# The residual rows stored to memory ahead of the experts, and added to there by each expert's scatter

## The chip, the cores and the metric

The program runs on one core of one Trainium2 chip. The time is device microseconds of that core, launch to end of one execution. Measured before the change: a median of 1953.42 us in 3 runs (1949.82 to 1957.47).

## The reference

Two layers (DEPTH = 2) over x, 256 tokens by 2048 numbers, float32. Each layer is an attention part and a mixture of experts (MoE):

```python
x = x + mixed @ w_out[l]
x = x + moe_ffn(rms_norm(x, ffn_norm[l]), w_router, router_bias, w_gate[l], w_up[l], w_down[l])
```

The MoE has 16 experts. The router picks 2 of them for each token, both from one group of 4 experts. An expert computes `silu(h @ wg) * (h @ wu)`, scaled by the token's gate value, and then `@ wd`. A token's result is its x plus the outputs of its two experts. One expert's weights are 3 x 2048 x 512 floats, 12.6 MB; a layer's 16 experts are 201 MB.

## The kernel before, in words

Each layer first streams the weights of the input projection and the output projection through TensorE (PE), with the attention heads worked in between. It ends with the new x in SBUF (tile `x`, two tiles of 128 tokens by 2048) and the normalised rows in `rows`. POOL stores these to memory (`expert_rows`, L508).

Then comes the expert stage, `one_round`. It is written out by hand as a list of steps for each engine.

- SP issues the weight loads (`load`, L460), 192 loads of 1 MB a layer, into a ring of 8 buffers: four in `raw`, four in `proj`. A load waits on `lo_ready`, that is, until both halves of what its buffer held have been cut. The first 8 loads of the stage go out before the attention part has ended.
- Every half buffer is cut into a high part by ACT (L590) and a low part by VectorE (DVE, L1232), and PE multiplies with both (L1032, L1034, L1051 to L1053). So one expert takes 24 cuts on ACT, 24 on DVE and 24 groups of matmuls on PE.
- A round has 64 places (SLOTS) for each expert. POOL gathers an expert's rows from `expert_rows` by the table `tok_at` (L514) and later scatters its results with `put_at` (L522). A row of 2048 numbers is handled as two rows of 1024 (4 KB), so each gather and scatter has 128 places; those without a token point out of bounds and move nothing. With 256 tokens and two picks each, a mean of 32 of an expert's 64 places are filled.
- The scatters write into the tensor `picks`, of 2 x 256 rows: the first picks of all tokens and then the second picks. A row has one writer. 14 of the 16 experts scatter; the last two are joined in SBUF by a matmul (`join`, L1079) and added to `x` from PSUM by `add_last` (L1746). In the attention part POOL fills `picks` with x_in (L499), so that every row holds finite numbers.
- At the end of the stage POOL waits for the sixth and then for the last of the final 8 weight loads (`raw_landed5`, `raw_landed7`) and loads `picks` back, four tiles of 1 MB (L560). DVE multiplies each by a mask (`in_round`, which leaves out rows not written) and adds it to `x` (`add_picks`, L1737), four instructions one after another, each pair behind its own semaphore. Then come the four `add_last(j)`, each waiting for `joined`. Each counts `x_cols` up, and the next layer's transposes of x (L891), or the stores of the output (SP, L482), wait for that.

`Tally.due` computes the count that a wait must see. `x_ready` is raised when x of the attention part is complete (DVE, after L1349). SP's last wait of a layer is on `picks_landed1`.

Of the kernel before, what the change touches and what calls it, by code (L numbers as in the profile page):

```python
# [16 lines left out]
F32 = mybir.dt.float32  # L17
F32R = mybir.dt.float32r
I32 = mybir.dt.int32
U32 = mybir.dt.uint32  # L20
# [145 lines left out]
def shape_constants():  # L166
# [29 lines left out]
    "raw_landed5": (0, 2 * NE * EXP_UNITS), "raw_landed7": (0, 2 * NE * EXP_UNITS), "picks_filled": (32, 0), "picks_landed0": (0, 16 * NT), "picks_landed1": (0, 16 * NT), "last_out": (0, 4),  # L196
# [120 lines left out]
def trunk(nc, x_in, in_units, forget_w, out_units, expert_units, norms, small_in, const_in, router_in,  # L317
          rows_dram, picks_dram, out):
    with ExitStack() as ctx:
        def sb(name, shape, dt=F32):  # L320
            return ctx.enter_context(nc.sbuf_tensor(name, shape, dt))
# [33 lines left out]
        in_round = sb("in_round", [P, 2, NT])  # L355
# [3 lines left out]
        put_at = sb("put_at", [P, NE, 1], U32)  # L359
# [35 lines left out]
        picked = [spare[:, 4 * D:5 * D], spare[:, 5 * D:6 * D], rows[:, 0, :], wide[:, :]]  # L395
# [51 lines left out]
        def _(e):  # L447
# [15 lines left out]
            for layer in t_.layers():  # L463
                with t_.loop(e.Fori(0, IN_UNITS // RAW)) as i:
                    load(in_units, layer * IN_UNITS + i * RAW)
                with t_.loop(e.Fori(0, OUT_UNITS // RAW)) as i:
                    load(out_units, layer * OUT_UNITS + i * RAW)
                e.wait_ge(S["proj_free"], t_.due("proj_free"))
                t_.fence()
                with t_.one_round():  # L470
                    load(expert_units, layer * (NE * EXP_UNITS), DEEP)
                    with t_.loop(e.Fori(1, NE * EXP_UNITS // DEEP)) as i:
                        load(expert_units, layer * (NE * EXP_UNITS) + i * DEEP, DEEP, DEEP)
                    t_.decide()
                    e.wait_ge(S["picks_landed1"], t_.due("picks_landed1", 16 * NT))
                    t_.fence()
# [10 lines left out]
        def _(e):  # L487
            t_ = tally(e, start={"out_ready": 1},
                       counted=("xt_banked", "out_ready", "scattered0", "scattered1"))
            for layer in t_.layers():  # L490
# [5 lines left out]
                e.wait_ge(S["dT_ready"], t_.due("dT_ready"))  # L496
                t_.fence()
                for k in range(2):
                    e.dma_start(picks_dram[k * SEQ:(k + 1) * SEQ, :], x_in).then_inc(S["picks_filled"], 16)  # L499
# [10 lines left out]
                e.wait_ge(S["picks_filled"], t_.due("picks_filled", 32))  # L510
# [8 lines left out]
                def scatter(k):  # L519
                    e.wait_ge(S["out_ready"], t_.due("out_ready"))  # L520
                    t_.fence()
                    e.indirect_dma_start(picks_dram.rearrange("r (h n) -> (r h) n", h=2),  # L522
                                         bass.IndirectOffsetOnAxis(ap=put_at[:, k, :], axis=0),
                                         expert_out[k % 2], None,
                                         bounds_check=4 * SEQ - 1, oob_is_err=False)\
                        .then_inc(S[f"scattered{k % 2}"], 16)
# [7 lines left out]
                with t_.one_round():  # L534
                    e.wait_ge(S["tables_ready"], t_.due("tables_ready"))
                    t_.fence()
                    gather(0)
                    gather(1)
                    for k in range(NE + 1):
                        if k < NE:  # L540

                            e.wait_ge(S["xt_banked"], t_.due("xt_banked", 2))
                            t_.fence()
                        if k + 2 == FIRST:
                            e.wait_ge(S["tables_ready"], t_.due("tables_ready"))
                            t_.fence()
                        if k + 2 < NE:
                            gather(k + 2)
                        if k >= 3:
                            freed(k - 3)  # L550
                        if 2 <= k < LAST + 2:
                            scatter(k - 2)
                    t_.decide()
                    for k in range(2 * NT):
                        if k % NT == 0:

                            slot = f"raw_landed{DEEP - 3 + k}"
# [658 lines left out]
        def _(e):  # L1216
# [92 lines left out]
            for layer in t_.layers():  # L1309
# [317 lines left out]
                for k in (4, 5):  # L1627
# [10 lines left out]
                    if k == 4:  # L1638
# [14 lines left out]
                v.scalar_tensor_tensor(out=info[:, :, :, 1], in0=R(5), scalar=float(2 * SEQ), in1=token,  # L1653
                                       op0=ALU.mult, op1=ALU.add)
# [45 lines left out]
                def tables(a, b):  # L1700
# [4 lines left out]
                    for side in range(2):  # L1705
# [5 lines left out]
                        v.tensor_scalar(put_at[s, a:c, 0], found[:, 0:c - a, 1], NOWHERE + side, None, ALU.add)  # L1711
# [4 lines left out]
                def last_tables():  # L1716

                    for t in range(NT):
                        v.tensor_copy(back[t], bank[4][:, (1 + t) * P:(2 + t) * P])
                    v.tensor_copy(last_weight[SLOTS:STACK, :], bank[4][SLOTS:STACK, 4 * NE:4 * NE + 4])  # L1720
                    place = route[:, 3, :, :].unsqueeze(1).to_broadcast([P, 2, NT, NE])
                    inside = route[:, 0:2, :, :]
# [8 lines left out]
                    e.wait_ge(S["dve_done"], t_.due("dve_done"))  # L1731

                def add_picks(k):

                    e.wait_ge(S[f"picks_landed{k}"], t_.due(f"picks_landed{k}", 16 * NT))
                    for t in range(NT):
                        v.scalar_tensor_tensor(out=x[:, t, :], in0=picked[NT * k + t],  # L1737
                                               scalar=in_round[:, k, t:t + 1], in1=x[:, t, :],
                                               op0=ALU.mult, op1=ALU.add).then_inc(S["dve_done"], 1)

# [43 lines left out]
                with t_.one_round():  # L1784
# [94 lines left out]
```

## Time and profile before

| | |
|---|---|
| median of 3 runs | 1953.42 us |
| profiled execution, its own time | 1956.39 us |
| its span in the trace | 1954.2 us |
| mean granted TensorE clock | 0.974 |
| PE busy | 1848.6 us, 95% |
| DVE busy | 1581.5 us, 81% |
| ACT busy | 1438.5 us, 74% |
| POOL busy | 104.6 us, 5% |
| DMA queue of SP (q1) | 542.01 MB, 70.4% of 16 engines |
| DMA queue of POOL (q0) | 38.95 MB, 5.3% |

The shares are means over the whole span. The two expert stages run from about 465 to 970 us and from about 1430 to 1940 us, and in them all three compute engines and the 16 DMA engines are over 90% busy at once. Which one sets the pace has to be read from smaller stretches.

### The profile page before, as it was taken

What the parts mean: (1) busy time and instruction counts of PE and PEld (TensorE: products, weight loads), DVE (VectorE), ACT (ScalarE), POOL (GpSimd) and SP (SyncE); (2) the same over time, 40 slices, a digit from 0 to 9 for tenths busy, and PEclk for the clock granted to TensorE, in tenths of its full rate; (3) what the DMA queues carried; (4) which work ended last, traced back from release to release, by engine and by line L of the source; (5) the groups of instructions that cost most, each with busy time, mean ns of one, the idle gap of its engine ahead of it and who ended that gap; (6) DMA issues with size and microseconds to landing.
All of it is one profiled execution on the core that took longest, in us unless ns stands there. A gap on an engine that the chain in (4) does not pass through costs nothing.

```text
span 1954.2 us, 30129 instructions
## 1 busy us (share of the span) xinstructions
PE 1848.6 (95%) x8762; PEld 1494.0 (76%) x8762; DVE 1581.5 (81%) x2248; ACT 1438.5 (74%) x2279; POOL 104.6 (5%) x86
## 2 busy tenths in 40 slices
PE   7999999997999999989999999999979999999998
PEld 6887888886677777778778878888867777777775
DVE  5566777657999999999974667775589999999998
ACT  5465666445899999899765646664468999999995
POOL 0000000001010111000000000000010110100000
PEclk9999999996999999999999999999979999999999
DMA  7654444565999999999856444345569999999997
GB/s 271 212 186 141 161 162 155 183 230 201 380 420 420 421 422 421 422 421 419 346 209 243 155 151 161 141 173 194 215 237 409 420 421 421 421 420 418 421 420 270
DMA packets 86699, 582.07 MB, mean 298 GB/s; under 512 B 13612, under 2 KB 13868, under 8 KB 18896
## 3 DMA queue, kind: packets, MB, share of 16 engines
q1 hardware_dynamic: 75600, 542.01, 70.4%
q0 software_dynamic: 11008, 38.95, 5.3%
q8 instruction: 45, 0.74, 0.1%
q14 instruction: 46, 0.38, 0.1%
HBM read 575.91 MB, written 29.36 MB: 310 GB/s over the span
## 4 chain that ended last, share of the span: by engine, by line
PE 58%; DMA 14%; DVE 10%; issue 10%; ACT 7%; ACTq 0%; DVEq 0%; SPq 0%; POOL 0%; POOLq 0%
PE bank L877 12%; PE bank L879 11%; PE bank L878 11%; DMA proj<-in_expert_units 8%; DMA raw<-in_expert_units 5%; PE bank L1032 4%; PE bank L1034 4%; DVE wl L1232 3%; ACT wh L590 3%; PE bank L1051 2%; PE bank L1053 2%; PE bank L1052 2%; DVE xl L1232 2%; PE bank L1023 2%; ACT rows L807 1%
## 5 line engine op out<-in xcount | busy, mean ns | idle before, releaser
L1224 DVE TENSOR_TENSOR wl<-raw,wh 128x1024 fp32r<-128x1024 f32 x256 | 310.1, 1222 | 229.9 <-ACT wh L581 229.6
L581 ACT ACTIVATE wh<-raw 128x1024 fp32r<-128x1024 f32 x256 | 269.0, 1056 | 268.5 <-PE bank L879 266.3
L877 PE MATMUL bank<-wh,xh 128*128 128x512 f32 x1024 | 417.1, 407 | 2.5 <-DVE wl L1224 2.4
L879 PE MATMUL bank<-wh,xl 128*128 128x512 f32 x1024 | 403.3, 394 | 0.0
L878 PE MATMUL bank<-wl,xh 128*128 128x512 f32 x1024 | 401.8, 392 | 0.0
L1232 DVE TENSOR_TENSOR wl<-raw,wh 128x1024 fp32r<-128x1024 f32 x256 | 301.2, 1218 | 22.3 <-ACT wh L590 22.0
L1232 DVE TENSOR_TENSOR wl<-proj,wh 128x1024 fp32r<-128x1024 f32 x256 | 300.6, 1217 | 14.9 <-ACT wh L590 14.6
L590 ACT ACTIVATE wh<-raw 128x1024 fp32r<-128x1024 f32 x256 | 260.0, 1052 | 30.3 <-PE bank L1053 11.6
L590 ACT ACTIVATE wh<-proj 128x1024 fp32r<-128x1024 f32 x256 | 260.5, 1052 | 22.1 <-PE bank L1053 11.0
L1032 PE MATMUL bank<-wh,xh 128*128 128x512 f32 x648 | 267.7, 413 | 4.9 <-DVE xh L1672 3.0
L1034 PE MATMUL bank<-wl,xh 128*128 128x512 f32 x648 | 259.9, 401 | 0.0
L877 PEld LDWEIGHTS bank<-wh,xh 128*128 128x128 f32 x1024 | 194.2, 190 | 47.4 <-issue 8.3
L879 PEld LDWEIGHTS bank<-wh,xl 128*128 128x128 f32 x1024 | 193.9, 189 | 43.4
L878 PEld LDWEIGHTS bank<-wl,xh 128*128 128x128 f32 x1024 | 194.6, 190 | 36.7
L1232 DVE TENSOR_TENSOR xl<-raw,xl 128x1024 fp32r<-128x1024 f32 x128 | 153.0, 1216 | 3.4 <-ACT xl L590 3.2
L1232 DVE TENSOR_TENSOR xl<-proj,xl 128x1024 fp32r<-128x1024 f32 x128 | 152.8, 1216 | 3.2 <-ACT xl L590 3.0
L1032 PEld LDWEIGHTS bank<-wh,xh 128*128 128x128 f32 x648 | 125.7, 194 | 37.8 <-DVE wl L1232 7.0
L1032 PE MATMUL bank<-xl,xh 128*128 128x512 f32 x376 | 147.8, 393 | 2.5 <-DVE xl L1232 2.5
L1051 PE MATMUL bank<-wh,actT 128*128 128x512 f32 x360 | 146.5, 407 | 3.2 <-DVE actT L1690 2.1
L1034 PE MATMUL bank<-xl,xh 128*128 128x512 f32 x376 | 146.6, 390 | 0.0
L1034 PEld LDWEIGHTS bank<-wl,xh 128*128 128x128 f32 x648 | 125.6, 194 | 24.7
L1053 PE MATMUL bank<-wh,actT 128*128 128x512 f32 x360 | 142.3, 395 | 0.0
(258 smaller groups left out, 2720.8 us busy)
## 6 DMA issues: line engine op xcount, KB each, us to landing
raw<-in_expert_units SPq DMA_DIRECT2D x192, 1024.0 KB, 13.7
proj<-in_expert_units SPq DMA_DIRECT2D x192, 1024.0 KB, 14.2
raw<-in_in_units SPq DMA_DIRECT2D x96, 1024.0 KB, 4.9
raw<-in_out_units SPq DMA_DIRECT2D x32, 1024.0 KB, 4.8
expert_rows<-rows POOLq DMA_DIRECT2D x4, 1024.0 KB, 4.5
proj<-picks POOLq DMA_DIRECT2D x4, 1024.0 KB, 7.9
x<-in_x SPq DMA_DIRECT2D x2, 1024.0 KB, 7.3
wide<-in_norms POOLq DMA_DIRECT2D x2, 1024.0 KB, 4.9
```

What stands on the lines that cost most here:

```text
L581: act_(wh[:, h % CUT, :], ring[j][:, h % 2 * HALF:(h % 2 + 1) * HALF], ACT.Copy)\
L590: act_(high[part_slot(h, kind)], ring[j][:, h % 2 * HALF:(h % 2 + 1) * HALF], ACT.Copy)\
L877: mm(out, xh[:, at, tok], rh, start=start, stop=False)
L878: mm(out, xh[:, at, tok], rl, start=False, stop=False)
L879: return mm(out, xl[:, at, tok], rh, start=False, stop=stop)
L1023: last = mm(bank[6][:, at + k * SLOTS:at + (k + 1) * SLOTS], wide_act[:, k * P:(k + 1) * P], cst("fold"), start=True, stop=True)
L1032: mm(bank[m][:, :], stacked[b][:, 2 * h + c, :], high[j][:, k], start=(h + c == 0), stop=False)
L1034: last = mm(bank[m][:, :], stacked[b][:, 2 * h + c, :], low[j][:, k], start=False, stop=(h == PART - 1 and c == 1))
L1051: mm(o, left_of[:, k, 0:STACK], high[j][:, r], start=(k == 0), stop=False)
L1053: last = mm(o, left_of[:, k, SLOTS:SLOTS + STACK], high[j][:, r], start=False, stop=(k == 3))
L1224: v.tensor_tensor(wl[:, h % CUT, :], ring[(first + h // 2) % slots][:, h % 2 * HALF:(h % 2 + 1) * HALF], wh[:, h % CUT, :].bitcast(F32), A ...
L1232: v.tensor_tensor(low[j], ring[(at + h // 2) % DEEP][:, h % 2 * HALF:(h % 2 + 1) * HALF], high[j].bitcast(F32), ALU.subtract).then_inc(S[" ...
```

## The change

x is stored to a memory tensor `sums` by SP, after the first 8 weight loads of the expert stage, once x is complete. Each expert's scatter adds its rows to `sums` (`compute_op=ALU.add`) in place of writing them to a row of their own. At the end of the stage POOL loads `sums` back into `x`, two tiles of 1 MB, and DVE has only the joined rows of the last two experts to add. The fill of `picks`, the mask `in_round`, the second index table `put_at` and `add_picks` go. The first scatter waits for the store of x.

```diff
@@ SP
                     load(expert_units, layer * (NE * EXP_UNITS), DEEP)
+                    e.wait_ge(S["x_cols"], t_.ahead("x_cols", 0) + 8)
+                    e.wait_ge(S["x_ready"], t_.ahead("x_ready", 2 * NT))
+                    for t in range(NT):
+                        e.dma_start(sums_dram[t * P:(t + 1) * P, :], x[:, t, :]).then_inc(S["x_stored"], 16)
                     with t_.loop(e.Fori(1, NE * EXP_UNITS // DEEP)) as i:
                         load(expert_units, layer * (NE * EXP_UNITS) + i * DEEP, DEEP, DEEP)
                     t_.decide()
-                    e.wait_ge(S["picks_landed1"], t_.due("picks_landed1", 16 * NT))
+                    e.wait_ge(S["sums_landed"], t_.due("sums_landed", 16 * NT))
@@ POOL
-                e.wait_ge(S["dT_ready"], t_.due("dT_ready"))
-                t_.fence()
-                for k in range(2):
-                    e.dma_start(picks_dram[k * SEQ:(k + 1) * SEQ, :], x_in).then_inc(S["picks_filled"], 16)
...
                 def scatter(k):
                     e.wait_ge(S["out_ready"], t_.due("out_ready"))
+                    if k == 0:
+                        e.wait_ge(S["x_stored"], t_.due("x_stored", 16 * NT))
                     t_.fence()
-                    e.indirect_dma_start(picks_dram.rearrange("r (h n) -> (r h) n", h=2),
-                                         bass.IndirectOffsetOnAxis(ap=put_at[:, k, :], axis=0),
+                    e.indirect_dma_start(sums_dram.rearrange("r (h n) -> (r h) n", h=2),
+                                         bass.IndirectOffsetOnAxis(ap=tok_at[:, k, :], axis=0),
                                          expert_out[k % 2], None,
-                                         bounds_check=4 * SEQ - 1, oob_is_err=False)\
+                                         bounds_check=2 * SEQ - 1, oob_is_err=False, compute_op=ALU.add)\
                         .then_inc(S[f"scattered{k % 2}"], 16)
...
-                    for k in range(2 * NT):
-                        if k % NT == 0:
-
-                            slot = f"raw_landed{DEEP - 3 + k}"
-                            e.wait_ge(S[slot], t_.due(slot, 16 * NE * EXP_UNITS // DEEP))
-                            t_.fence()
-                        e.dma_start(picked[k], picks_dram[k * P:(k + 1) * P, :])\
-                            .then_inc(S[f"picks_landed{k // NT}"], 16)
-                    for k in range(2):
-                        e.wait_ge(S[f"picks_landed{k}"], t_.due(f"picks_landed{k}", 16 * NT))
+                    slot = f"raw_landed{DEEP - 3}"
+                    e.wait_ge(S[slot], t_.due(slot, 16 * NE * EXP_UNITS // DEEP))
+                    t_.fence()
+                    for t in range(NT):
+                        e.dma_start(x[:, t, :], sums_dram[t * P:(t + 1) * P, :]).then_inc(S["sums_landed"], 16)
+                    e.wait_ge(S["sums_landed"], t_.due("sums_landed", 16 * NT))
@@ VectorE
-                v.scalar_tensor_tensor(out=info[:, :, :, 1], in0=R(5), scalar=float(2 * SEQ), in1=token,
-                                       op0=ALU.mult, op1=ALU.add)
+                v.tensor_copy(info[:, :, :, 1], token)
...
-                        v.tensor_scalar(put_at[s, a:c, 0], found[:, 0:c - a, 1], NOWHERE + side, None, ALU.add)
...
-                    v.scalar_tensor_tensor(out=inside, in0=place, scalar=0.0, in1=route[:, 4:6, :, :],
-                                           op0=ALU.is_ge, op1=ALU.mult).then_inc(S["dve_done"], 1)
-                    e.wait_ge(S["dve_done"], t_.due("dve_done"))
-                    v.scalar_tensor_tensor(out=inside, in0=place, scalar=float(SLOTS), in1=inside,
-                                           op0=ALU.is_lt, op1=ALU.mult).then_inc(S["dve_done"], 1)
-                    e.wait_ge(S["dve_done"], t_.due("dve_done"))
-                    v.tensor_reduce(in_round[:, :, :], inside[:, :, :, 0:LAST], AX, ALU.add)\
-                        .then_inc(S["dve_done"], 1)
...
-                    add_picks(0)
-                    e.wait_ge(S["dve_done"], t_.due("dve_done", NT))
-                    add_picks(1)
-                    e.wait_ge(S["dve_done"], t_.due("dve_done", NT))
+                    e.wait_ge(S["sums_landed"], t_.due("sums_landed", 16 * NT))
                     for j in range(4):
                         add_last(j)
```

## Rows read from the trace of the kernel before

**Rows 1.** Windows of the expert stages: engines' busy us, granted clock, DMA share, GB/s
```profile
657.08:687.55 30.47, 29.38 (x137) 23.29 (x136) 29.64 (x30) 28.70 (x36) 3.56 (x3) 1.00 1.01 420
...
843.07:875.37 32.30, 29.07 (x131) 23.29 (x130) 30.16 (x30) 29.06 (x36) 2.74 (x3) 0.95 1.01 422
...
500.00:948.00 448.00, 425.44 (x1960) 339.76 (x1958) 429.65 (x420) 414.47 (x504) 42.15 (x26) 0.99 1.01 419
1465.00:1914.00 449.00, 424.40 (x1971) 339.48 (x1969) 432.31 (x422) 415.77 (x505) 39.38 (x26) 1.00 1.01 419
```

**Rows 2.** Weight loads (L460) issued in 535 to 566 us, then 811 to 843
```profile
DMA to landing us min/median/max: 7.7/8.7/9.5
...
DMA to landing us min/median/max: 15.8/17.0/18.0
```

**Rows 3.** Waits in 811 to 843 us: total, times, longest
```profile
ACT wh L590 <- DMA raw<-in_expert_units: 1.4, 2, 1.1
```

**Rows 4.** POOL's queue (packets, MB, share): 500-948, 1465-1914, 875-907, 84-104 us
```profile
q0 software_dynamic: 3744, 7.38, 4.3%
...
q0 software_dynamic: 3744, 6.63, 3.9%
...
q0 software_dynamic: 144, 0.25, 2.1%
...
q0 software_dynamic: 96, 4.19, 60.6%
```

**Rows 5.** DMA issues of the whole span: count, KB each, median us to landing
```profile
proj<-picks POOLq DMA_DIRECT2D x4, 1024.0 KB, 7.9
...
picks<-rows,put_at POOLq DMA_INDIRECT x28, 7.9
...
const<-in_const SPq DMA_DIRECT2D x1, 96.0 KB, 2.0
```

**Rows 6.** Timeline ahead of the first expert stage: SP, then DVE
```profile
428.84 2.12 SPq L460 DMA_DIRECT2D proj<-in_expert_units  x4
465.72 2.97 SPq L460 DMA_DIRECT2D raw<-in_expert_units  x2
...
441.10 1.29 DVE L1349 TENSOR_TENSOR x<-bank,x 128x512 f32<-128x512 f32 x2 [5.53 <-PE bank L879]
```

**Rows 7.** Windows behind x's completion in either layer, columns as in rows 1
```profile
442.50:453.20 10.70, 7.12 (x40) 7.01 (x40) 7.83 (x35) 5.43 (x11) 0.00 (x0) 0.58 0.02 7
...
1413.00:1418.00 5.00, 4.72 (x25) 4.51 (x24) 3.33 (x16) 0.95 (x3) 0.00 (x0) 0.55 0.00 0
```

**Rows 8.** Timeline of the tail of layer 0: PE, DVE, POOL
```profile
972.01 7.03 PE L1079 MATMUL bank<-rows,qkT 128*128 128x512 f32 x16
...
982.34 1.09 PE L891 MATMUL bank<-const,x 128*128 128x128 f32 x8 [2.43 <-DVE x L1746]
...
968.02 4.60 DVE L1737 SCALAR_TENSOR_TENSOR x<-proj,in_round,x 128x2048 f32<-128x2048 f32 x2
...
977.41 4.87 DVE L1746 TENSOR_TENSOR x<-bank,x 128x512 f32<-128x512 f32 x8
...
957.22 1.15 POOL L560 DMA_DIRECT2D proj<-picks  x2 [18.63 <-DMA proj<-in_expert_units]
```

**Rows 9.** Timeline of the tail of layer 1: PE, DVE
```profile
1937.85 7.03 PE L1079 MATMUL bank<-rows,qkT 128*128 128x512 f32 x16
...
1944.06 4.87 DVE L1746 TENSOR_TENSOR x<-bank,x 128x512 f32<-128x512 f32 x8
```

**Rows 10.** Timeline of the first expert of layer 0: DVE, then PE
```profile
487.75 0.21 DVE L1729 TENSOR_REDUCE in_round<-qkT 128x4 f32<-128x56 f32 x1
...
490.26 0.50 PE L1032 MATMUL bank<-wh,xh 128*128 128x512 f32 x1 [0.93 <-DVE wl L1232]
```

**Rows 11.** Windows around the fill and at layer 1's start, columns as in rows 1
```profile
84.00:104.00 20.00, 20.00 (x100) 16.24 (x99) 12.12 (x19) 13.84 (x30) 1.02 (x2) 1.00 0.88 304
984.00:990.00 6.00, 5.97 (x16) 4.58 (x17) 6.00 (x10) 3.39 (x7) 0.00 (x0) 0.50 0.55 193
```

More of the change, by code:

```diff
@@ L195 @@
     "gain_landed": (16, 0), "small_landed": (32, 0), "rows_stored": (16 * NT, 0),
-    "raw_landed5": (0, 2 * NE * EXP_UNITS), "raw_landed7": (0, 2 * NE * EXP_UNITS), "picks_filled": (32, 0), "picks_landed0": (0, 16 * NT), "picks_landed1": (0, 16 * NT), "last_out": (0, 4),
+    "raw_landed5": (0, 2 * NE * EXP_UNITS), "raw_landed7": (0, 2 * NE * EXP_UNITS), "x_stored": (0, 16 * NT), "sums_landed": (0, 16 * NT), "last_out": (0, 4),
     "joined": (0, 4), "x_ready": (2 * NT, 0), "x_cols": (4, 4), "sq_ready": (HA + HC, 0), "gains_ready": (1, 0), "rows_squared": (2, 0),
@@ L317, in trunk @@
 def trunk(nc, x_in, in_units, forget_w, out_units, expert_units, norms, small_in, const_in, router_in,
-          rows_dram, picks_dram, out):
+          rows_dram, sums_dram, out):
     with ExitStack() as ctx:
@@ L354, in trunk @@
         out_stat = sb("out_stat", [P, 3, NT, NH])
-        in_round = sb("in_round", [P, 2, NT])
         more = sb("more", [1, 2])
@@ L358, in trunk @@
         tok_at = sb("tok_at", [P, NE, 1], U32)
-        put_at = sb("put_at", [P, NE, 1], U32)
         turned_qk = qkT[:, :, :, :].rearrange("p a b n -> p (a b n)")
@@ L394, in trunk @@
         gathered = [spare[:, 4 * D + b * HALF:4 * D + (b + 1) * HALF] for b in range(2)]
-        picked = [spare[:, 4 * D:5 * D], spare[:, 5 * D:6 * D], rows[:, 0, :], wide[:, :]]
         last_rows = rows[SLOTS:STACK, 1, :]
@@ L509, in _ @@
                 e.wait_ge(S["rows_stored"], t_.due("rows_stored", 16 * NT))
-                e.wait_ge(S["picks_filled"], t_.due("picks_filled", 32))
                 t_.fence()
@@ L1720, in last_tables @@
                     v.tensor_copy(last_weight[SLOTS:STACK, :], bank[4][SLOTS:STACK, 4 * NE:4 * NE + 4])
-                    place = route[:, 3, :, :].unsqueeze(1).to_broadcast([P, 2, NT, NE])
-                    inside = route[:, 0:2, :, :]
-                    v.scalar_tensor_tensor(out=inside, in0=place, scalar=0.0, in1=route[:, 4:6, :, :],
-                                           op0=ALU.is_ge, op1=ALU.mult).then_inc(S["dve_done"], 1)
-                    e.wait_ge(S["dve_done"], t_.due("dve_done"))
-                    v.scalar_tensor_tensor(out=inside, in0=place, scalar=float(SLOTS), in1=inside,
-                                           op0=ALU.is_lt, op1=ALU.mult).then_inc(S["dve_done"], 1)
-                    e.wait_ge(S["dve_done"], t_.due("dve_done"))
-                    v.tensor_reduce(in_round[:, :, :], inside[:, :, :, 0:LAST], AX, ALU.add)\
-                        .then_inc(S["dve_done"], 1)
[L1731 to L1739, printed above, removed]
                 def add_last(j):
@@ L1873 @@
     rows_dram = nc.dram_tensor("expert_rows", (SEQ, D), F32, kind="Internal").ap()
-    picks_dram = nc.dram_tensor("picks", (2 * SEQ, D), F32, kind="Internal").ap()
+    sums_dram = nc.dram_tensor("sums", (SEQ, D), F32, kind="Internal").ap()
     out = nc.dram_tensor("out_rows", (SEQ, D), F32, kind="ExternalOutput").ap()
-    trunk(nc, *args, rows_dram, picks_dram, out)
+    trunk(nc, *args, rows_dram, sums_dram, out)
     r = run(nc, [arrays], core_ids=[0])
```

## The prediction

> **What bounds the kernel now.** The page says that PE is busiest. But the change touches the expert stages and their tails, so I cut these into windows of one expert each, between POOL's scatters, and read busy time and DMA share side by side. An expert early in the stage takes 30.47 us, with DVE busy for 29.64 and PE for 29.38. A late one takes 32.30 us, while its DVE and PE work has not grown. The DMA share is 1.01 in both and over the whole stage, at 419 to 422 GB/s, so the DMA engines never run dry [rows 1].
>
> A full share alone doesn't say that DMA is the bound, since a queue with a backlog also looks full. So the next view is the weight loads' time from issue to landing. It grows from 8.7 us to 17.0 us, and there it stops [rows 2]. The ring explains the stop. It has 8 buffers of 1 MB; an expert uses 12 of them in 30.47 us, 2.54 us each; 8 x 2.54 = 20.3 us, less the time in which a buffer is being cut (about one buffer's 2.54 us and a little more), leaves some 17. In the first part the engines set the pace and DMA falls behind a little with every expert, living off the ring's reserve. When the reserve is used up the engines wait for weights: ACT, which never did before, now waits for loads [rows 3]. By then everything depends on when the DMA engines have done all their work of the stage.
>
> That gives the rule for this change. **In the expert stage each microsecond of additional DMA work, at any expert, moves the end of the stage by one microsecond**, and each microsecond saved on PE, ACT or DVE inside it is worth almost nothing. In the tail, behind the last weights, it is the reverse: DVE's adds and PE's join set the end.
>
> **The change part by part.**
>
> *The scatter with an add.* 14 scatters a layer. The POOL queue took 4.3% of 448 us = 19.3 us of all 16 engines in layer 0, and 3.9% of 449 us = 17.5 us in layer 1 [rows 1, 4]. In each of these stretches there are 26 indirect transfers (12 gathers, 14 scatters), so one costs (19.3 + 17.5) / 52 = 0.71 us. The stretch that holds a single scatter gives nearly the same, 2.1% of 31.4 us = 0.66 us for 0.25 MB [rows 4]. The 28 plain scatters thus cost 28 x 0.71 = 19.8 us of DMA work now. The trace shows no transfer that adds, so its price must be bounded. Below: the read of the old row might run beside the engine's other traffic and cost nothing, 0. Above: each row might have to wait for a whole round trip before the next starts. The shortest lone transfer takes 2.0 us from issue to landing [rows 5]. A scatter has 0.25 MB / 4 KB = 64 filled rows, 4 for each of 16 engines, 8 us a scatter, +224 us in all. Between them is the nearest row for what is new, 4 KB read from memory for each 4 KB written: the memory-to-memory fill took 60.6% of 20 us = 12.1 us for 4.19 MB, 2.9 us a MB, against 0.66 / 0.25 = 2.6 us a MB for the plain scatter [rows 4]. The additional read is as many bytes again, so I take the price of as many bytes again, **+19.8 us**. I choose this and not the far end since each of these transfers keeps many rows in flight: the fill moves 4.19 MB in 12 us, which would not be possible at 2 us for each row of an engine.
>
> The Trainium skill (Collectives: The Full Stack, "The bandwidth ceiling: the fold count and why AG ≠ RS ≠ AR") says that a transfer with an add emits two reads for one write on the same ring and so runs at about half the rate of a copy, measured ratio 1.93. By that the term would be 0.93 x 19.8 = 18.4 us in place of 19.8, and the time 1.4 us less. No row here shows a transfer with an add.
>
> Nothing else waits for a scatter. Its buffer is needed again two experts later, and the next scatter but one, 30 us on, is the first thing held up, while the landing now takes 7.9 us [rows 1, 5].
>
> *The store of x.* 2.1 MB on SP's queue, 2.1 / 0.42 = 5.0 us of DMA work. On paper it is in front of the ninth weight load, but SP's last of the first 8 loads goes out at 428.84 + 2.12 = 430.96 us and the ninth only at 465.72; x is complete at 441.10 + 1.29 = 442.4 [rows 6]. From there until the store of the normalised rows the DMA engines are idle, share 0.02 for 10.7 us, and 0.00 at the same place in layer 1 [rows 7]. So it costs nothing. If that cover were gone it would be +5.0 us a layer.
>
> *The fill of `picks`* (L499) goes. Its 12 us of DMA time were hidden: PE was busy for 20.00 of the 20 us around it [rows 11]. 0.
>
> *VectorE in the first expert.* The three instructions that make `in_round` go, the last of them 0.21 us long, some 0.8 us with their waits and the short ones on `put_at`. PE waited 0.93 us for DVE just behind [rows 10]. The DMA backlog isn't there yet, so earlier cuts release buffers earlier. I take half, -0.5 us a layer (bounds 0 and -0.9), **-1.0 us**.
>
> *The tail.* DVE added the picks from 968.02 and began `add_last` at 977.41, done 4.87 us later, at 982.28. PE's join ran from 972.01 to 979.04 [rows 8]. Four joins in 7.03 us are 1.76 each, so DVE can do its j-th add (4.87 / 4 = 1.22 us) as they come, and the last ends at 979.04 + 1.22 = 980.3: **-2.0 us**. In layer 1, 1937.85 + 7.03 + 1.22 = 1946.1 against 1944.06 + 4.87 = 1948.93 [rows 9]: **-2.8 us**; the output stores follow the last add. Is the sum there in time? The two loads go out at the same place as the first two of before, 957.22 us, and took 7.9 us [rows 5, 8]: about 965, 9 us before the first joined columns. What is late next is the join on PE itself, behind the last weights. SP's first loads of the next layer go out earlier, but PE at that point waits for DVE (2.43 us in front of L891 [rows 8]), so no gain beyond the 2.0.
>
> *The sum.* +19.8 - 1.0 - 2.0 - 2.8 = +14.0 us. The profiled execution, 1956.4 us (span 1954.2 and 2.2 around it), becomes 1970.4. It lay 3.0 us above the median of the runs, so the median goes from 1953.4 to **1967.4**; I say 1967.
>
> **Rivals.**
>
> *The add's read is hidden* (not slower). If the engines' write side sets the rate and reads run beside it, only the gains are left: 1953.4 - 5.8 = 1947.6. For it: a scatter's 0.71 us isn't taken apart by the trace. Against it: the DMA share of 1.01 leaves no slack to put a read into. It decides if an adding scatter costs less than about 0.9 us.
>
> *The add is slower than two passes.* If an adding row costs four times a plain one, +59.4 us in place of 19.8: 1953.4 + 59.4 - 5.8 = 2007. For it: nothing bounds the adder's own rate. Full serial waiting would give 1953.4 + 224 - 5.8 = 2172; the scatter would then land after 16 us and more, still inside the 30 us it has.
>
> *The tail gives more.* PE's granted clock is at 0.50, the 1.2 GHz level, for 6 us at the start of layer 1 [rows 11], after the 2.43 us wait for DVE. If the shorter gap keeps it at 2.4 GHz, 6 x 0.5 = 3 us more are won in layer 0; with a hidden read, 1944.6.
>
> *The store of x collides* with loads after all: +10, 1977.
>
> **How the numbers follow.** Two passes: 0.53, own range 1960 to 1976. Hidden read: 0.22 (with the better tail 0.05 of it). Slower than two passes: 0.20, of which 0.04 beyond 2007. Collision: 0.05. The range runs from the hidden read with some spread to just below the four-fold price: 1946 to 2003; it leaves out about 0.07 below and 0.08 above. 0.5% is 9.8 us, about what a measurement of this kernel can tell from no change. Below 1943.6 lies only the best end of the hidden read, 0.04. Within 1943.6 to 1963.2 lie the rest of it and the low edge of the two passes, where an add costs up to 1.5 times as much: 0.29. Slower: 0.67.
>
> **What would show it.** Right: POOL's queue share in the expert stages near 6.5% in place of 4.3%; weight loads reaching their 17 us about two experts earlier; late experts 0.7 us longer; the last cut of layer 0 some 9 us later; DMA idle before 453 us but for the store; no L1737, and L1746 in step with L1079. Wrong: an expert stage of the same length (hidden read); experts over 34 us, or `freed` waits on POOL (slow add); weight loads late at 466 us (store). The prediction fails by its size if an adding scatter is far from 1.4 us of DMA work.

## The result, and the profile after

The changed kernel takes a median of 1961.49 us (20 runs, 1954.57 to 1965.85) against 1951.8 us of the kernel before (20 runs). The ratio is 1.0044 [1.0037, 1.0052], so +8.6 us (7.2 to 10.1); the two medians lie 9.7 us apart. It is slower, and the interval leaves no doubt about the sign, but the size lies just inside the 0.5% that the prediction drew as its bound. 1967 was predicted.

The profiled execution took 1962.92 us, span 1961.0, granted clock 0.971. That is 6.8 us of span more than the profiled one of before, which lay 4.6 us above its kernel's median, where this one lies 1.4 above. Differences of whole spans are therefore good to a few us only; what follows rests on stretches. In the page of after, the queues and the DMA issues:

```profile
q1 hardware_dynamic: 76176, 546.21, 70.4%
q0 software_dynamic: 10240, 26.37, 4.4%
...
raw<-in_expert_units SPq DMA_DIRECT2D x192, 1024.0 KB, 15.5
...
sums<-x SPq DMA_DIRECT2D x4, 1024.0 KB, 5.7
...
x<-sums POOLq DMA_DIRECT2D x4, 1024.0 KB, 7.8
```

POOL's queue moves 12.6 MB less than before (26.37 against 38.95), and yet its share falls only from 5.3% to 4.4%. In time of 16 engines these are 103.6 and 86.3 us, 17.3 less. The fill alone took 2 x 12.1 us [rows 4], and half of the picks' 8.4 MB at 0.42 MB a us another 10. So 34 us went and 17 came, 0.6 for each of the 28 scatters. That can be seen where they run. Windows (columns as in [rows 1]) from the first scatter of a stage to its last, 13 experts, for layer 0 and layer 1 in after; and from the third last scatter of layer 0 to the second last:

```profile
532.59:943.97 411.38, 385.44 (x1758) 309.16 (x1759) 388.80 (x377) 375.83 (x456) 43.49 (x25) 0.98 1.01 412
1505.41:1915.21 409.80, 385.26 (x1765) 309.98 (x1766) 389.19 (x377) 376.04 (x456) 41.28 (x24) 0.98 1.01 412
880.25:913.24 32.99, 30.60 (x138) 24.60 (x137) 30.27 (x30) 29.02 (x36) 1.59 (x2) 0.95 1.01 407
```

The queue of POOL in the same three windows:

```profile
q0 software_dynamic: 3456, 6.78, 6.3%
...
q0 software_dynamic: 3456, 5.96, 5.7%
...
q0 software_dynamic: 144, 0.25, 3.9%
```

The same windows of before, with the queue behind the first and then behind the second:

```profile
535.25:937.61 402.36, 382.14 (x1760) 305.59 (x1760) 387.19 (x377) 375.08 (x456) 38.64 (x24) 0.99 1.01 421
1502.58:1904.94 402.36, 380.09 (x1767) 304.58 (x1767) 387.56 (x377) 375.89 (x456) 35.88 (x25) 1.00 1.01 420
...
q0 software_dynamic: 3456, 6.77, 4.4%
q0 software_dynamic: 3456, 5.96, 3.9%
```

Read them as one sum. Packets and megabytes of the queue are the same, although each row is now read as well, so the profile counts only what a scatter writes. Its DMA time is not the same: 4.4% of 402.36 is 17.7 us, 6.3% of 411.38 is 25.9 us, 8.2 us more for 13 scatters. In layer 1 it is 15.7 and 23.4, 7.7 us more. The windows grew by 9.0 and 7.4 us. DVE and ACT did the same work, the DMA share stays at 1.01, and the recorded rate falls from 421 to 412 GB/s. The DMA engines are busy with something that the megabytes don't show, and the stage pays for it about one to one. A lone scatter shows it as well: 3.9% of 32.99 us = 1.29 us for 0.25 MB, against 0.66 us before [rows 4].

The weight loads (L457), issued in 532.59 to 562.95, then 684.8 to 716.1, in us from issue to landing, and who waited for them in the second stretch:

```profile
DMA to landing us min/median/max: 8.9/10.1/11.3
...
DMA to landing us min/median/max: 14.8/16.7/17.7
...
  ACT wh L584: 2.8, 4
```

In the kernel before, ACT's waits and a median of 17 us came late in the stage [rows 2, 3]; here both are there by 700 us. The starts of the scatters say the same. Their distance is about 30.46 us for five experts, up to 684.80, and the next is 31.30. Before, it kept that pace for eight experts, up to 778.93. In layer 1 it now holds for four experts (to 1627.17) and did for six (to 1685.34). The additional work first uses up the ring's reserve, unseen, and comes out once that is gone.

Now the tail. PE, DVE and POOL around the join of layer 0 in after:

```profile
978.54 7.03 PE L1073 MATMUL bank<-rows,qkT 128*128 128x512 f32 x16
985.40 1.04 PE L885 MATMUL bank<-const,x 128*128 128x128 f32 x8
986.95 1.09 PE L885 MATMUL bank<-const,x 128*128 128x128 f32 x8 [0.51 <-DVE x L1718]
...
980.46 1.29 DVE L1718 TENSOR_TENSOR x<-bank,x 128x512 f32<-128x512 f32 x2 [5.82 <-PE bank L1073]
...
985.61 1.29 DVE L1718 TENSOR_TENSOR x<-bank,x 128x512 f32<-128x512 f32 x2 [0.43 <-PE bank L1073]
...
964.91 1.18 POOL L556 DMA_DIRECT2D x<-sums  x2 [19.41 <-DMA proj<-in_expert_units]
```

`add_last` (L1718) now goes in step with the join and ends at 986.90, 1.3 us behind it, where DVE ended 3.2 us behind [rows 8]. By the median time to landing, 7.8 us, the sum was there at about 973, 7 us before it was needed. One more thing moved. The window that answers to the last of [rows 11]:

```profile
984.00:990.00 6.00, 4.48 (x25) 2.89 (x24) 4.85 (x9) 3.89 (x8) 0.00 (x0) 1.00 0.51 202
```

The granted clock is 1.00 there, the 2.4 GHz level, where it was 0.50. PE's wait in front of L885 is 0.51 us in place of 2.43. The traces of all thirteen kernels of this study, cut into short windows behind the join of layer 0, say the same. In the four with a wait of 0.51 us here the granted clock stays at 1.00. In the nine with a wait of 2.2 us or more it goes to 0.50 for about 3 to 10 us, which costs 1.7 to 5.1 us of full-speed time. In before it costs 3.4 us, 2.4 of them behind the start of the next layer's matmuls at 985.07.

The end of layer 1 in after, DVE and SP:

```profile
1955.78 1.29 DVE L1718 TENSOR_TENSOR x<-bank,x 128x512 f32<-128x512 f32 x2 [0.43 <-PE bank L1073]
...
1951.95 5.96 SPq L483 DMA_DIRECT2D out_rows<-x  x8
```

The last add ends at 1957.07 and the span 3.9 us later. Before, it was 5.3 us from 1948.93 [rows 9] to 1954.2. The eight output stores, in before and in after, from issue to landing:

```profile
DMA to landing us min/median/max: 2.5/3.7/4.5
...
DMA to landing us min/median/max: 2.5/3.1/3.3
```

DVE now waits for each join, so its pairs of adds end 1.72 us apart in place of 1.22, and the stores go out further apart. That the last ones land sooner for this reason is likely; no run tests it by itself.

With the starts of the first scatter, the join and POOL's store of the normalised rows (453.27 and 1421.52 before, 452.52 and 1425.27 after) the whole difference of the spans can be put together:

| stretch | before | after | difference |
|---|---|---|---|
| start to rows stored, layer 0 | 453.27 | 452.52 | -0.75 |
| rows stored to first scatter, layer 0 / 1 | 81.98 / 81.06 | 80.07 / 80.14 | -1.9 / -0.9 |
| first scatter to join, layer 0 / 1 | 436.76 / 435.27 | 445.95 / 443.31 | +9.2 / +8.0 |
| join of layer 0 to rows stored, layer 1 | 449.51 | 446.73 | -2.8 |
| join of layer 1 to the end | 16.35 | 12.28 | -4.1 |
| sum | | | +6.8 |

The -2.8 holds -4.3 from the tail and +1.5 from a dip of PE's clock at 1142 to 1192 us, 0.94 against 0.97. Nothing in the change lies there, so I take this for scatter between executions. The 1.5 is an estimate, 0.03 of 50 us.

### The profile page after: what moved, and what is told of

Its sections match the earlier page's. It is cut to its first block, busy times and chain, and to the rows that moved or that the text cites. A ratio compares the mean times of both kernels' runs of the same rounds, so it can differ in the third digit from the quotient of the medians.

```text
span 1961.0 us, 30089 instructions
## 1 busy us (share of the span) xinstructions
PE 1854.8 (95%) x8762; PEld 1501.1 (77%) x8762; DVE 1565.4 (80%) x2226; ACT 1439.3 (73%) x2279; POOL 112.8 (6%) x78
## 3 DMA queue, kind: packets, MB, share of 16 engines
q0 software_dynamic: 10240, 26.37, 4.4%
## 4 chain that ended last, share of the span: by engine, by line
PE 59%; DMA 16%; DVE 9%; issue 8%; ACT 7%; ACTq 0%; DVEq 0%; SPq 0%
PE bank L871 12%; PE bank L873 11%; PE bank L872 11%; DMA raw<-in_expert_units 9%; DMA proj<-in_expert_units 6%; PE bank L1026 4%; PE bank L1028 4%; ACT wh L584 3%; DVE wl L1226 3%; PE bank L1045 3%; PE bank L1047 3%; PE bank L1046 3%; DVE xl L1226 2%; PE bank L1017 2%; ACT rows L801 1%
## 5 line engine op out<-in xcount | busy, mean ns | idle before, releaser
L584 ACT ACTIVATE wh<-proj 128x1024 fp32r<-128x1024 f32 x256 | 260.3, 1052 | 31.8 <-DMA proj<-in_expert_units 18.9
L1045 PE MATMUL bank<-wh,actT 128*128 128x512 f32 x360 | 146.9, 408 | 3.0 <-DVE actT L1683 2.1
L1046 PE MATMUL bank<-wl,actT 128*128 128x512 f32 x360 | 142.6, 396 | 0.0
```

What stands on the lines that cost most here:

```text
L584: act_(high[part_slot(h, kind)], ring[j][:, h % 2 * HALF:(h % 2 + 1) * HALF], ACT.Copy)\
L1045: mm(o, left_of[:, k, 0:STACK], high[j][:, r], start=(k == 0), stop=False)
L1046: mm(o, left_of[:, k, 0:STACK], low[j][:, r], start=False, stop=False)
```

## The experiments

All ratios are to the kernel before, run beside them on the same chip. Microseconds behind a ratio are the ratio applied to the median of before.

**The add alone, in the kernel before.**

```diff
                     e.indirect_dma_start(picks_dram.rearrange("r (h n) -> (r h) n", h=2),
...
-                                         bounds_check=4 * SEQ - 1, oob_is_err=False)\
+                                         bounds_check=4 * SEQ - 1, oob_is_err=False, compute_op=ALU.add)\
```

> The kernel before with the add alone: each scatter into picks adds to the row it finds, in place of overwriting it (so a pick comes back with the filled row added to it). Nothing else is changed: no store of x, the same tail with four adds on VectorE. My theory, two passes of DMA work for one: the changed kernel's trace shows POOL's queue about 17 us busier over both expert stages, so +15 to +20 us, ratio 1.008 to 1.010, with the weight loads reaching 17 us to landing one or two experts earlier. Rival, the add is nearly free and the changed kernel lost its time elsewhere (the store of x, the order of the tail): 1.000 to 1.002. Rival, the add is slow by itself: over 1.015.

Measured: 1971.12 us, 1.0104 [1.0086, 1.0121], +20.3 us (16.8 to 23.6). Its groups on POOL, and its queue from the first scatter to the last, 412.78 us:

```profile
L522 POOL DMA_INDIRECT picks<-rows,put_at x28 | 44.6, 1594 | 468.7 <-ACT rows L807 468.7
...
q0 software_dynamic: 3456, 6.78, 6.4%
```

The prediction's term of +19.8 us for 28 adding scatters stands, with nothing else of the change in play. (The sums are wrong in this kernel, so layer 1 works on other tokens; the stretch shown is of layer 0, where the data are the same.) The instruction on POOL also grows, from 1.00 to 1.59 us, which nobody waits for. A scatter lands after 9.0 us in place of 7.9.

**The change without the add.** A first version only took `compute_op` away.

```diff
-                                         bounds_check=2 * SEQ - 1, oob_is_err=False, compute_op=ALU.add)\
+                                         bounds_check=2 * SEQ - 1, oob_is_err=False)\
```

> The changed kernel with plain scatters, which overwrite the row of sums in place of adding to it (so x and the first pick are lost where a token has a second). All the rest of the change is kept: the store of x, one load back, the short tail, fewer VectorE instructions. My theory: the gains of the prediction alone, -5.8 us, and the 3 us of TensorE's clock at the start of layer 1 which the changed kernel's trace shows to have been kept, so -6 to -9 us, ratio 0.9955 to 0.997. Rival, the store of x costs 5 us a layer: 1.000 to 1.002.

Measured: 2454.85 us, 1.2582 [1.2558, 1.2605]. This says nothing of the change. With another x, layer 1 sent its tokens elsewhere, and a further round of experts was run (POOL's gathers start again at 1938.62 us), as happens when one expert gets more than its 64 places. The mended version keeps to one round:

```diff
-                    v.tensor_scalar(again[0:1, 0:1], more[0:1, 0:1], 0.0, None, ALU.is_gt)\
+                    v.tensor_scalar(again[0:1, 0:1], more[0:1, 0:1], 1e6, None, ALU.is_gt)\
```

> The changed kernel with plain scatters again (they overwrite rows of sums, so parts of the sum are lost), and with the question for a further round always answered no, since a wrong x sends the tokens of layer 1 to other experts. All of the change but the add: the short tail, the store of x, fewer VectorE instructions in the first expert. My theory: add alone +20.4, whole change +8.6, so the rest is -10 to -12 us, ratio 0.994 to 0.996. By the prediction's own terms -5.8 us: 0.997. Rival, the store of x costs 5 us a layer and the effects aren't additive: over 0.998.

Measured: 1940.37 us, 0.9947 [0.9931, 0.9963], -10.4 us (-13.5 to -7.2). Its window from the first scatter to the last in layer 0:

```profile
529.48:931.76 402.28, 382.08 (x1760) 305.81 (x1761) 387.14 (x377) 375.16 (x456) 38.69 (x25) 0.99 1.01 421
```

With plain scatters the window is that of the kernel before (402.36), to 0.1 us. So the 9.1 us between 402.28 and 411.38 are the add's, 0.70 a scatter. In layer 1, where this kernel computes with other data, it is 9.35 (400.45 against 409.80), 0.72. The rest of the change is worth 10 us, not the 5.8 that the prediction gave it (the interval, 7.2 to 13.5, leaves 5.8 out).

**A second plain scatter for each.** The first goes to `picks` as before, the second to a tensor `twin` that nothing reads.

```diff
-                    e.indirect_dma_start(picks_dram.rearrange("r (h n) -> (r h) n", h=2),
+                    for to in (picks_dram, twin_dram):
+                        e.indirect_dma_start(to.rearrange("r (h n) -> (r h) n", h=2),
```

> The kernel before with each scatter issued twice, the second to a tensor of the same size that nobody reads. It measures the price of a plain scatter, and whether DMA work in the expert stage moves the end one to one. My theory: 28 x 0.71 = +19.8 us, ratio 1.009 to 1.011, about what the add alone costs. Rival, the DMA engines have slack and the add costs by latency: this one is near 1.000 while the add alone is not.

Measured: 1976.44 us, 1.0134 [1.0116, 1.0151], +26 us. The queue's share from the first to the last first-of-two, 534.55 to 946.44:

```profile
q0 software_dynamic: 5328, 9.83, 6.2%
```

6.2% of 411.89 is 25.5 us, 7.8 more than before for 13 scatters, 0.60 each; the add cost 0.63. The window grew by 9.5 us against 9.0. So an add has the price of one more plain scatter, in DMA time and in the window alike. The recorded rate in that window stays at 420 GB/s, since here the additional bytes are counted. The whole time shows more than was expected, 26 us (23 to 29) against 20 (17 to 24) for the add alone, and the runs of the two don't overlap (1976.2 and more against 1973.0 and less). In the profiled executions the stages, from the store of the rows to the load of the picks, are longer than before by 22.0 us here and by 18.9 with the add alone. That is 3 of the 5 to 6 us. What the rest is stays open.

**No scatters at all.** POOL raises the semaphore itself, and the picks hold what the fill left.

```diff
-                    e.indirect_dma_start(picks_dram.rearrange("r (h n) -> (r h) n", h=2),
...
+                    e.sem_inc(S[f"scattered{k % 2}"], 16)
```

> The kernel before without any scatter (the experts' rows are left out of the sum, except the last two experts'). It takes 19.8 us of DMA work away. My theory, two bounds in turn: the gain ends where the engines' pace takes over; 13 experts took 402.4 us and would take 13 x 30.47 = 396.1, so about -6.3 us a layer, ratio 0.993 to 0.995, and ACT hardly waits for weights. Rival, DMA work is the only bound of the stage: -19.8 us, 0.990. Rival, DMA is not the bound at all: 1.000.

Measured: 1937.36 us, 0.9925 [0.9908, 0.9942], -14.6 us. POOL's gathers, one for each expert, and then the landing of the loads issued in 816 to 847, late in the stage, and a window from its second pair of gathers on:

```profile
516.75 2.52 POOL L514 DMA_INDIRECT proj<-expert_rows,tok_at  x1 [29.16 <-PE bank L1012]
547.19 2.54 POOL L514 DMA_INDIRECT proj<-expert_rows,tok_at  x1 [27.93 <-PE bank L1012]
...
DMA to landing us min/median/max: 10.2/11.1/11.6
...
485.30:821.34 336.04, 321.53 (x1488) 254.05 (x1487) 326.61 (x326) 313.79 (x383) 27.30 (x13) 1.00 1.01 415
```

The gathers stay some 30.5 us apart up to the last, at 851.80, and the landing is at 11 us where it was at 17 [rows 2]. ACT waits for no load there. This stage is bound by its engines, and its DMA share is 1.01 all the same: here the share cannot tell the two apart, the landing can. Taking 19.8 us of DMA work away brought 14.6 (11.3 to 17.9), since the bound changed hands on the way: 13 experts at the engines' own pace of 30.46 us are 396.0 us, and only 6.4 less than the 402.36 of before in each layer. Adding the same brought the full 20. That is the asymmetry of a stage that stands just past the point where both are equal.

**The old tail put back into the changed kernel.** Two more loads of `sums` behind the last weights, and four adds of DVE on spare memory ahead of `add_last`.

```diff
+                    slot = f"raw_landed{DEEP - 1}"
+                    e.wait_ge(S[slot], t_.due(slot, 16 * NE * EXP_UNITS // DEEP))
+                    for t in range(NT):
+                        e.dma_start((rows[:, 0, :], wide[:, :])[t], sums_dram[t * P:(t + 1) * P, :])\
+                            .then_inc(S["spare_landed"], 16)
...
+                            v.scalar_tensor_tensor(out=spare[:, (4 + t) * D:(5 + t) * D], in0=x[:, t, :],
+                                                   scalar=0.5, in1=(rows[:, 0, :], wide[:, :])[t] if k else x[:, t, :],
+                                                   op0=ALU.mult, op1=ALU.add).then_inc(S["dve_done"], 1)
```

> The changed kernel with the old tail put back beside the new one: POOL loads sums a second time into two spare tiles behind the last weights, and VectorE does four additions of the old size and kind into spare memory, two behind each pair of loads, before the first joined columns are added. The output is unchanged. It measures what the short tail is worth in the changed kernel. My theory from the two traces: 2 us less from the join to the first matmuls of layer 1, 2.4 us of TensorE's clock kept there, and 2.7 + 1.3 us at the end of layer 1, together 8.3 us (the prediction said 4.8), so against the kernel before +17 us, ratio 1.0075 to 1.0095. Rival, the tail is worth only the 4.8 us of the prediction: 1.006 to 1.007.

Measured: 1971.73 us, 1.0096 [1.008, 1.0112], +18.7 us; the change itself has +8.6. So the short tail is worth 10 us, give or take about 3 (its parts in the traces, 4.3 and 4.1, make 8.4). DVE and then two windows of this kernel (granted clock third from the end):

```profile
973.86 4.50 DVE L1782 SCALAR_TENSOR_TENSOR proj<-x 128x2048 f32<-128x2048 f32 x2 [1.36 <-DMA x<-sums]
...
983.82 4.87 DVE L1726 TENSOR_TENSOR x<-bank,x 128x512 f32<-128x512 f32 x8
...
987.00:990.00 3.00, 1.25 (x6) 1.25 (x7) 2.27 (x5) 2.48 (x5) 0.00 (x0) 0.67 1.04 434
990.00:993.00 3.00, 3.00 (x12) 2.30 (x11) 3.00 (x5) 3.00 (x6) 0.00 (x0) 0.50 0.57 238
```

With DVE late again, PE waits 2.49 us for it and the clock falls to 0.50, the 1.2 GHz level, as in the kernel before. That ties the kept clock to the short tail.

**x stored twice.** A second copy goes to `twin`, also ahead of the ninth load.

```diff
+                    for t in range(NT):
+                        e.dma_start(twin_dram[t * P:(t + 1) * P, :], x[:, t, :]).then_inc(S["x_stored"], 16)
```

> The changed kernel with x stored twice, the second time to a tensor that nobody reads, both in front of the ninth weight load on SP. The output is unchanged. My theory: the DMA engines are idle there for over 10 us and two stores need about that, so it costs at most 1 us a layer against the changed kernel, ratio to the kernel before 1.004 to 1.0055. Rival, a store of x costs its 5 us of DMA time in each layer: 1.009 to 1.010.

Measured: 1961.31 us, 1.0045 [1.0028, 1.0062], the time of the change. SP in this kernel:

```profile
441.94 0.82 SPq L472 DMA_DIRECT2D sums<-x  x2
442.81 2.33 SPq L474 DMA_DIRECT2D twin<-x  x2
464.64 13.29 SPq L457 DMA_DIRECT2D raw<-in_expert_units  x4
```

Both stores are issued almost 20 us before the ninth load. Against the change, a second store costs 0.2 us, and at most about 4: the store costs nothing that these runs can tell.

**Can the gain be had without the add?** Four versions of the kernel before. First, its mask `in_round` is made earlier, in a gap of DVE within the first expert (at 471 us in place of 487); nothing else moves.

```diff
-                    v.tensor_reduce(in_round[:, :, :], inside[:, :, :, 0:LAST], AX, ALU.add)\
...
                                 rows_lo(0, g, (7, 5)[g])
+                            mask_picks()
```

> The kernel before with one edit: the three VectorE instructions that make in_round run earlier, in a gap of VectorE in the first expert. The output is unchanged. It measures what is saved of VectorE's work ahead of a stage that DMA bounds later. Prediction's term: -0.5 us a layer, ratio 0.9995. From the changed kernel's trace, where the second pair of gathers went out 1 us earlier relative to the stage's start: up to -1 us a layer, 0.999. Rival, the moved instructions only delay something else there: 1.000 to 1.001.

Measured: 1951.53 us, 0.9996 [0.9985, 1.0007]. The first scatter came 2.0 and 1.0 us earlier behind the store of the rows, as in the changed kernel (79.98 and 80.03 us), and the whole gained at most 3 us.

Second, GpSimd multiplies and adds one of the four pick tiles, to shorten DVE's tail (the early mask is in it too).

```diff
+                    nc.gpsimd.tensor_scalar(picked[1], picked[1], in_round[:, 0, 1:2], None, ALU.mult)\
+                        .then_inc(S["pool_added"], 1)
+                    e.wait_ge(S["pool_added"], t_.due("pool_added"))
+                    nc.gpsimd.tensor_tensor(x[:, 1, :], picked[1], x[:, 1, :], ALU.add)\
```

> The kernel before with plain scatters kept, aimed at the gains without the cost: GpSimd, idle in the tail, multiplies and adds one of the four pick tiles, so that VectorE is through when the last join ends; and the three instructions that make in_round move to a gap of VectorE in the first expert. The output is unchanged. My theory: VectorE's queue in the tail is 2.3 us shorter, so the last add moves up to the end of the join; -8 us for both tails with the clock kept, and -1 to -2 us in the first experts: ratio 0.995 to 0.996. Rival, GpSimd's two operations take over 9 us or slow VectorE down, and the tail stays as it was: 0.999 to 1.002.

Measured: 1959.27 us, 1.0037 [1.0021, 1.0053], slower. POOL, then DVE:

```profile
963.93 10.36 POOL L564 TENSOR_SCALAR proj<-proj,in_round 128x2048 f32<-128x2048 f32 x1 [3.34 <-DMA proj<-picks]
974.47 4.58 POOL L568 TENSOR_TENSOR x<-proj,x 128x2048 f32<-128x2048 f32 x1 [0.18 <-POOL proj L564]
...
969.09 5.61 DVE L1749 SCALAR_TENSOR_TENSOR x<-rows,in_round,x 128x2048 f32<-128x2048 f32 x1
979.09 2.35 DVE L1749 SCALAR_TENSOR_TENSOR x<-wide,in_round,x 128x2048 f32<-128x2048 f32 x1 [4.39 <-POOL x L568]
```

GpSimd needed 15 us for what DVE does in 2.35, and DVE then waited 4.39 us for it.

Third and fourth: the picks are filled with zeros, so that no mask is needed, and the tile is added by GpSimd or all four by DVE.

```diff
-                    e.dma_start(picks_dram[k * SEQ:(k + 1) * SEQ, :], x_in).then_inc(S["picks_filled"], 16)
+                    e.dma_start(picks_dram[k * SEQ:(k + 1) * SEQ, :], zeros_in).then_inc(S["picks_filled"], 16)
...
+                    nc.gpsimd.tensor_tensor(x[:, 1, :], picked[1], x[:, 1, :], ALU.add)\
```

> The kernel before with plain scatters; picks is filled with zeros, so no mask is needed (this gives the right sum as long as one round is enough, as here), in_round goes, and GpSimd adds one of the four pick tiles with one plain addition in place of the two operations of the last attempt. My theory: that attempt's trace shows 4.6 us for GpSimd's addition, 7.5 and 10.4 us for its multiplication and VectorE slowed down beside the multiplication. With the addition alone GpSimd is through at 969 us, before VectorE needs the tile at 972.7: the last add ends with the join, ratio 0.995 to 0.997. Rival, GpSimd's addition slows VectorE's cuts and adds beside it as the multiplication did: 0.999 to 1.002.

> The same with all four additions on VectorE: zeros in picks, no mask, plain additions. Against the run with GpSimd it tells what GpSimd's part is worth. My theory: an addition of 128x2048 takes VectorE as long as the masked one (2.34 us), so only the first expert's 1 us a layer is saved: ratio 0.999 to 1.000. Rival, a plain addition is shorter and the tail moves up: 0.997 to 0.998.

Measured: 1.0001 [0.9991, 1.001] with GpSimd, 0.9993 [0.9984, 1.0003] with DVE alone. With zeros the sum is right only as long as one round is enough, as it is here. No version of this study that gives the right result beats the kernel before by a measurable amount.

## Why the prediction held, and where its sizes were off

**The bound.** The prediction's rule was that each additional microsecond of DMA work in the expert stage moves its end by one. It held: 8.2 and 7.7 us more of POOL's queue against windows longer by 9.0 and 7.4. The picture behind it, DMA falling behind expert by expert on the ring's reserve, is shown by both sides: with more DMA work the pace slips three experts earlier in layer 0 and two in layer 1, and with none of the scatters it does not slip. One detail was wrong. "Late experts 0.7 us longer" gave each late expert its own price only. The five experts up to 684.80 pay nothing at once and the other eight all of it, 9.0 us, 1.1 each.

**The price of the add.** Predicted as the price of the same bytes once more, +19.8 us in 28 scatters. Measured: +20.3 us alone in the kernel before (16.8 to 23.6), 18.45 us for 26 scatters as the difference of the windows with and without it, 0.71 each, which is the predicted number, and 0.61 each by POOL's queue. The rivals of a hidden read and of an add slower than two passes are refuted. Serial waiting at 8 us a scatter is as well, since a scatter lands 1.2 us later than before and not 8. The prediction's reason against it was not sound, though. It took the fill for rows of 4 KB, but the fill's 4.19 MB went in 96 packets [rows 4], 44 KB each in the mean: six for each of 16 engines, which at 2.0 us each make the same 12 us. So that row did not speak on an add of small rows, and that its price per byte carried over is partly luck; the experiments are what settles it. The Trainium skill's rule for the reduce step of a collective (Collectives: The Full Stack, "The bandwidth ceiling: the fold count and why AG ≠ RS ≠ AR") is two reads for one write and about half the rate. Half the rate agrees with this trace, 1.29 us against 0.66 for a lone scatter; the number of reads no trace here shows.

**The step that was mis-sized** is the term of the gains, -5.8 us. Measured with plain scatters it is -10.4 us (-13.5 to -7.2), and the trace shows where its parts differ:

- Tail of layer 0: -4.3 in place of -2.0. The adds in step with the join gave -1.9, as worked out. The other 2.4 us are the kept clock. The prediction had it as a rival at 3 us and did not put it into its sum. Its own condition ("if the shorter gap keeps it at 2.4 GHz") was met, and the old tail put back took the clock away again.
- Tail of layer 1: -4.1 in place of -2.8. The last add came 2.7 us nearer to the join, as worked out. The output stores then ended 1.3 us sooner behind the last add; the prediction let them "follow the last add" unchanged.
- First experts: -1.9 and -0.9 in place of -0.5 each, up to the first scatter; layer 0 lies outside the prediction's bound of -0.9. I had halved the saving for no reason from the trace. The early mask alone brings the same 2.0 and 1.0 us up to there. How much of it lasts to the end isn't settled: its whole time is 0.9996 [0.9985, 1.0007], 0.8 us less, and the interval includes no gain at all.

The sum of predicted terms was +14.0. With the measured -10.4 in place of -5.8 it would have been 19.8 - 10.4 = +9.4, against +8.6 (7.2 to 10.1) measured.

**The store, the fill, the waits.** The store of x is at nothing, as predicted; a doubled store shows it. The fill has no run of its own; that it cost nothing rests on PE's full 20.00 us beside it [rows 11]. No wait on `freed` and none on the sum appeared (the prediction let the next scatter but one be the first held up; by the code of `freed` it is the next one, still 30 us on). The last cut of layer 0 came 6.5 us later (968.10 to 974.64) and not 9: the first expert's saving, the earlier start of the stage and a shorter catching up of the engines after the last weights stand against the 9.

**The chances.** The likeliest case came about, but its gains were larger, so that the time fell just inside the 0.5% that I had given 0.29 and not 0.67. The sign was right. The edge was also misread: by the prediction's own sum, 1963.2 is an add of 15.6 us on top of 19.8, 1.8 times a plain scatter and not 1.5, so more of the two passes belonged inside it.

## What to carry to other kernels

An add in memory cost here what one more pass of the same bytes over the DMA engines costs. In a stage that already lives off its ring's reserve that is a bad trade: 10 us of gains, most of them from the exposed tail, were bought for 19 us. Where the DMA engines have slack it may be a good one; no run here shows it. The order of the adds also has to be kept. In this kernel POOL waits in `freed` until one scatter has landed before it issues the next, which is free since they are 30 us apart and land after 9; what two adds to the same row at once would give was not tried. Whether a stage that shows a full DMA share really waits for DMA is read from the time from issue to landing against the depth of the ring, and from who waits. An experiment that removes work there understated the price of adding it (14.6 against 20 us). When a tail gets shorter, look at the clock on the far side of the gap and at what is queued behind the last instruction (2.4 and 1.3 us here).

## What the runs showed of the hardware

- Beside each other, GpSimd and VectorE slowed down. POOL and DVE of the version with the zero fill and GpSimd:

```profile
961.20 7.55 POOL L564 TENSOR_TENSOR x<-proj,x 128x2048 f32<-128x2048 f32 x1 [3.68 <-DMA proj<-picks]
...
962.05 2.28 DVE L1731 TENSOR_TENSOR x<-proj,x 128x2048 f32<-128x2048 f32 x1
965.96 4.93 DVE L1731 TENSOR_TENSOR x<-rows,x 128x2048 f32<-128x2048 f32 x1 [1.63 <-DMA wide<-picks]
```

  GpSimd's add took 7.55 us here and 4.58 where DVE waited for it. DVE's second add took 4.93 us; the first, at 962.05, kept its 2.28. The Trainium skill (SBUF — State Buffer, "SBUF: two separate sides") describes a pair of ports that one of the two holds for a whole instruction while the other is blocked. The second add fits that: from 965.96 to POOL's end at 968.75 is 2.8 us, and 2.28 more make 5.1, against 4.93. So does POOL's own length: from the end of DVE's first add, 964.33, its 4.58 us would end at 968.91, and it ended at 968.75. In the version that also multiplies it fits less well: DVE's 5.61 us end only 0.4 us after POOL's 10.36, where a whole add, 2.35, should follow.
- The profile counts an adding scatter with the bytes that it writes. What else it does shows in the queue's share (6.3% in place of 4.4%) and in the rate, 412 GB/s at a full share in place of 421: 9.0 us x 421 GB/s = 3.8 MB, and 13 scatters of 0.26 MB are 3.4 MB.
- The same scatter with an add occupies POOL for 1.59 us in place of 1.00.
- At the start of layer 1, behind a busy stretch, a wait of PE of 2.2 us or more was followed by about 3 to 10 us at the 1.2 GHz level in nine kernels, and one of 0.51 us by none in four.
